# First stage of a one-core decoder layer: x in four column pieces, the first weight chunk split by blocks, identity turns on TensorE ahead of the data

## What is computed

```python
def rmsnorm(x, w):
    xf = x.astype(jnp.float32)
    y = xf * lax.rsqrt(jnp.mean(xf * xf, axis=-1, keepdims=True) + EPS)
    return (y * w.astype(jnp.float32)).astype(x.dtype)
...
    h = x                                     # (1, 256, 2048)
    for l in range(DEPTH):                    # DEPTH = 1
        n = rmsnorm(h, attn_norm_w[l])
        proj = n @ w_in[l]                    # 2048 x 2672
        c_q, c_kv, k_rope, q_nsa, kv_cmp, kv_slc, kv_win, gate_logits = _split_cols(proj, IN_SIZES)
        y_mla = mla_attention(c_q, c_kv, k_rope, positions, ...)
        y_nsa = nsa_attention(q_nsa, kv_cmp, kv_slc, kv_win, gate_logits, ...)
        y = jnp.concatenate([rmsnorm(y_mla, mla_out_norm_w[l]),
                             rmsnorm(y_nsa, nsa_out_norm_w[l])], axis=-1)
        h = h + y @ w_o[l]
        n = rmsnorm(h, mlp_norm_w[l])
        h = h + jnp.square(jax.nn.relu(n @ w_up[l])) @ w_down[l]
    return rmsnorm(h, final_norm_w)
```

## Time and profile before

| what | value |
|---|---|
| median of 3 runs | 1125.73 us (1125.38 to 1125.78) |
| span of the profiled execution, first to last instruction | 1125.1 us |
| TensorE busy | 1091.2 us, 97% of the span |
| VectorE, ScalarE, GpSimd busy | 629.8, 490.7, 94.3 us |
| chain that ended last: TensorE, VectorE, ScalarE | 93%, 3%, 2% |
| DMA | 190.41 MB, 169 GB/s on average |
| mean granted TensorE clock | 0.991 |

### The profile page before, as it was taken

One profiled execution on the slowest core, in us unless ns is written; L12 is line 12 of the kernel. 1 busy time (PEld: TensorE's weight loads), 2 busy tenths in 40 slices (PEclk: granted clock), 3 DMA queues, 4 the chain that ended last, 5 costly groups with the idle time before them and its releaser, 6 DMA issues.

```text
span 1125.1 us, 14165 instructions
## 1 busy us (share of the span) xinstructions
PE 1091.2 (97%) x5544; PEld 893.2 (79%) x5544; DVE 629.8 (56%) x762; ACT 490.7 (44%) x591; POOL 94.3 (8%) x157
## 2 busy tenths in 40 slices
PE   5999899999999999999999999999999999999995
PEld 5889787766666888888888888888888888888784
DVE  3655855566564656546555554554545554654664
ACT  3655344655554454334433433433433433433433
POOL 2135100432121200000000000000000000000002
PEclk9999999899999999999999999999999999999998
DMA  8476563142222555666556655566665665665641
GB/s 295 152 205 204 161 222 102 49 150 76 75 76 82 180 171 176 198 193 194 188 188 186 186 186 186 188 189 187 192 195 185 197 189 190 190 187 186 186 150 75
DMA packets 81807, 190.41 MB, mean 169 GB/s; under 512 B 8598, under 2 KB 20972, under 8 KB 81388
## 3 DMA queue, kind: packets, MB, share of 16 engines
q1 hardware_dynamic: 81772, 189.93, 53.5%
HBM read 187.82 MB, written 2.10 MB: 169 GB/s over the span
## 4 chain that ended last, share of the span: by engine, by line
PE 93%; DVE 3%; ACT 2%; issue 1%; DMA 0%; DVEq 0%; SPq 0%; POOL 0%; ACTq 0%
PE ps L1430 21%; PE ps L1092 17%; PE ps L1093 16%; PE ps L1096 16%; PE ps L1432 11%; PE ps L1249 2%; PE ps L1296 2%; DVE w_lo L723 2%; PE ps L1270 2%; PE ps L1297 1%; PE ps L1247 1%; PE ps L1246 1%; ACT w_hi L506 1%; DMA x_sb<-in_x 0%; PE ps L1286 0%
## 5 line engine op out<-in xcount | busy, mean ns | idle before, releaser
L723 DVE TENSOR_TENSOR w_lo<-raw,w_hi 128x2048 fp32r<-128x2048 f32 (+3 forms) x197 | 405.6, 2062 | 373.4 <-ACT w_hi L513 296.7
L513 ACT ACTIVATE w_hi<-raw 128x2048 fp32r<-128x2048 f32 x120 | 230.2, 1918 | 399.8 <-PE ps L1096 202.1
L1430 PE MATMUL ps<-xT,w_hi 128*128 128x512 f32 x1024 | 361.8, 398 | 1.3 <-DVE h_sb L903 1.0
L1432 PE MATMUL ps<-xT,w_lo 128*128 128x256 f32 x1024 | 287.1, 280 | 0.0
L1430 PEld LDWEIGHTS ps<-xT,w_hi 128*128 128x128 f32 x1024 | 192.3, 188 | 49.2 <-issue 1.3
L1092 PE MATMUL ps<-w_hi,hidT 128*128 128x512 f32 x512 | 200.2, 391 | 2.4 <-issue 2.0
L1093 PE MATMUL ps<-w_lo,hidT 128*128 128x512 f32 x512 | 200.1, 391 | 0.0
L1432 PEld LDWEIGHTS ps<-xT,w_lo 128*128 128x128 f32 x1024 | 193.3, 189 | 0.5
L1096 PE MATMUL ps<-w_hi,hidT 128*128 128x512 f32 x512 | 158.2, 390 | 0.0
L506 ACT ACTIVATE w_hi<-raw 128x1024 fp32r<-128x1024 f32 (+3 forms) x77 | 107.1, 1397 | 85.1 <-PE ps L1096 61.9
L1092 PEld LDWEIGHTS ps<-w_hi,hidT 128*128 128x128 f32 x512 | 96.4, 188 | 23.4 <-issue 2.4
(11 more groups left out here) (245 smaller groups left out, 1021.3 us busy)
## 6 DMA issues: line engine op xcount, KB each, us to landing
raw<-in_w_up SPq DMA_DIRECT2D x64, 1024.0 KB, 5.3
raw<-in_w_down SPq DMA_DIRECT2D x64, 1024.0 KB, 5.5
raw<-in_w_o SPq DMA_DIRECT2D x16, 1024.0 KB, 5.5
raw<-in_w_in SPq DMA_DIRECT2D x8, 1024.0 KB, 5.0
raw<-in_w_in SPq DMA_DIRECT2D x8, 832.0 KB, 7.3
raw<-in_w_in SPq DMA_DIRECT2D x8, 816.0 KB, 4.5
raw<-in_mla_w_uq SPq DMA_DIRECT2D x12, 256.0 KB, 4.5
x_sb<-in_x SPq DMA_DIRECT2D x4, 512.0 KB, 7.0
```

The lines of the kernel that those rows point to most:

```text
L513: act.activation(w_hi[:, j % SPLIT, :], raw[:, j % RAW, :], ACT.Copy).then_inc(hi_done, 1)
L723: return dve.tensor_tensor(dst, src, high.bitcast(F32), ALU.subtract)
L1430: pe.matmul(ps[:, b0 + f, :].rearrange("p (c t) -> p c t", c=2), w_hi[:, slot, w], xT[:, :, k0 + b, :], start=start and b == 0, stop=False)
L1432: m = pe.matmul(ps[:, b0 + f, 0:T], w_lo[:, slot, w], xT[:, 0, k0 + b, :], start=False, stop=stop and b == 3)
```

## The change

SyncE now loads x in four pieces of 512 columns, each with its own semaphore: piece 0 ahead of chunk 0, piece c right after chunk c for c = 1, 2, 3. Chunk 0 is loaded as two DMAs, one for each block of 128 rows, with a semaphore each (`head_in`, and the usual `raw_in`). ScalarE and VectorE split chunk 0 in the same two blocks, between the blocks of x. TensorE has a new helper `keep_warm(n)`, which turns the identity n times into PSUM bank 3, a bank that the first products do not use; it is called with 4, 8 and 8. TensorE takes block 0 of chunk 0 as soon as `head_lo` and `xt_lo` allow and block 1 behind `lo_done`. The sums of squares move from rounds 3 and 4 to 5 and 6, since they need all four pieces, and VectorE's guess moves from round 5 to round 7. The arithmetic stays the same.

```diff
--- before.py
+++ after.py
@@ -210,11 +210,11 @@
-        x_in = sems("x_in0", "x_in1")
+        x_in = sems("x_in0", "x_in1", "x_in2", "x_in3")
         raw_in = sems(*[f"raw_in{n}" for n in range(RAW)])
         prm0_in, prm_in, cst_in, w2_in, h_in, fw_in, stored = sems("prm0_in", "prm_in", "cst_in", "w2_in", "h_in", "fw_in", "stored")
         hi_done, half_hi, lo_done, w_used, w_half = sems("hi_done", "half_hi", "lo_done", "w_used", "w_half")
-        first_done, = sems("first_done")
+        first_done, head_in, head_hi, head_lo = sems("first_done", "head_in", "head_hi", "head_lo")
         act_free, dve_free = sems("act_free", "dve_free")
         pool_c, dve_c = sems("pool_c", "dve_c")
         consts, warm, tables, prm_t, wcols_ok = sems("consts", "warm", "tables", "prm_t", "wcols_ok")
@@ -309,22 +309,28 @@
         @block.sync
         def _(sp):
             sp.dma_start(prm0[:, :], a["attn_norm_w"][0].rearrange("(r p) -> r p", p=P)).then_inc(prm0_in, 16)
-            for t in range(TT):
-                sp.dma_start(x_sb[:, t, 0:D // 2], x_rows[t][:, 0:D // 2]).then_inc(x_in[0], 16)
+            def load_x(q):
+                for t in range(TT):
+                    part = slice(512 * q, 512 * q + 512)
+                    sp.dma_start(x_sb[:, t, part], x_rows[t][:, part]).then_inc(x_in[q], 16)
+
+            load_x(0)
             for c in range(LOOP0):
                 if c >= RAW:
                     sp.wait_ge(lo_done, c - RAW + 1)
                 src, (b, w) = chunk(c)
                 dst = raw[:, raw_slot(c), 0:b * w].rearrange("p (b w) -> p b w", b=b)
-                if len(src) == 1:
+                if c == 0:
+                    for k, landed in enumerate((head_in, raw_in[raw_slot(0)])):
+                        sp.dma_start(dst[:, k, :], src[0][:, k, :]).then_inc(landed, 16)
+                elif len(src) == 1:
                     sp.dma_start(dst, src[0]).then_inc(raw_in[raw_slot(c)], 16)
                 else:
                     for k, piece in enumerate(src):
                         sp.dma_start(dst[:, k, :].rearrange("p (h e) -> p h e", h=piece.shape[1]), piece)\
                             .then_inc(raw_in[raw_slot(c)], 16)
-                if c == 0:
-                    for t in range(TT):
-                        sp.dma_start(x_sb[:, t, D // 2:D], x_rows[t][:, D // 2:D]).then_inc(x_in[1], 16)
+                if 1 <= c <= 3:
+                    load_x(c)
                 if c == RAW - 1:
                     for src, row, n in TABLE:
                         sp.dma_start(prm[row - KT:row - KT + n, :], src).then_inc(prm_in, 16)
@@ -521,18 +527,24 @@
                 act.activation(cT[:, 0, k, :], bank(k % 4, T), ACT.Copy,
                                scale=wcols[:, PRM["c"] + k:PRM["c"] + k + 1]).then_inc(ct_hi, 1)
 
+            def head_split_hi(b):
+                act.wait_ge(raw_in[raw_slot(0)] if b else head_in, 16)
+                act.activation(w_hi[:, split_slot(0), CW * b:CW * b + CW], raw[:, raw_slot(0), CW * b:CW * b + CW], ACT.Copy)\
+                    .then_inc(hi_done if b else head_hi, 1)
+
             act.wait_ge(wcols_ok, 1)
-            for c in range(8):
-                if c:
-                    split_hi(c)
+            x_hi(0)
+            head_split_hi(0)
+            x_hi(1)
+            head_split_hi(1)
+            for c in range(1, 8):
+                split_hi(c)
                 x_hi(2 * c)
                 x_hi(2 * c + 1)
-                if c == 0:
-                    split_hi(0)
-                if c in (3, 4):
-                    t = c - 3
-                    act.wait_ge(x_in[0], 16 * TT)
-                    act.wait_ge(x_in[1], 16 * TT)
+                if c in (5, 6):
+                    t = c - 5
+                    for q in range(4):
+                        act.wait_ge(x_in[q], 16 * TT)
                     if t:
                         act.wait_ge(ssq_ok, t)
                     act.activation(sink[:, :], x_sb[:, t, :], ACT.Square, accum_out=ssq[:, t:t + 1]).then_inc(ssq_ok, 1)
@@ -754,14 +766,17 @@
             dve.wait_ge(prm_t, 1)
             dve.tensor_copy(wcols[:, 0:KT], bank(7, KT)).then_inc(wcols_ok, 1)
             dve.wait_ge(wcols_ok, 1)
-            for c in range(8):
-                if c:
-                    split_lo(c)
+            for b in range(2):
+                x_lo(b)
+                dve.wait_ge(hi_done if b else head_hi, 1)
+                part = slice(CW * b, CW * b + CW)
+                low(w_lo[:, split_slot(0), part], raw[:, raw_slot(0), part], w_hi[:, split_slot(0), part])\
+                    .then_inc(lo_done if b else head_lo, 1)
+            for c in range(1, 8):
+                split_lo(c)
                 x_lo(2 * c)
                 x_lo(2 * c + 1)
-                if c == 0:
-                    split_lo(0)
-                if c == 5:
+                if c == 7:
                     dve.wait_ge(ssq_ok, 2)
                     link(dve.tensor_scalar(ssq[:, 0:2], ssq[:, 0:2], 1.0 / D, EPS, ALU.mult, ALU.add))
                     guess(r1[:, :], ssq[:, 0:2]).then_inc(guessed, 1)
@@ -1121,8 +1136,8 @@
                     pe.wait_ge(wcols_ok, 1)
                 if k >= 4:
                     pe.wait_ge(xt_lo, k - 3)
-                if k == KT // 2:
-                    pe.wait_ge(x_in[1], 16 * TT)
+                if k % 4 == 0:
+                    pe.wait_ge(x_in[k // 4], 16 * TT)
                 for t in range(TT):
                     m = pe.transpose(ps[:, 4 + k % 4, P * t:P * t + P], x_sb[:, t, P * k:P * k + P], ident[:, :])
                 m.then_inc(xt_t, 1)
@@ -1135,16 +1150,31 @@
                 m.then_inc(ct_t, 1)
 
 
+            def keep_warm(n):
+
+                for _ in range(n):
+                    pe.transpose(bank(3, P), ident[:, :], ident[:, :])
+
             pe.wait_ge(consts, 1)
-            pe.wait_ge(x_in[0], 16 * TT)
-            for k in range(3):
-                turn_x(k)
+            keep_warm(4)
             pe.wait_ge(prm0_in, 16)
             pe.transpose(bank(7, KT), prm0[:, :], ident[0:KT, 0:KT]).then_inc(prm_t, 1)
-            turn_x(3)
+            keep_warm(8)
+            for k in range(4):
+                turn_x(k)
+            keep_warm(8)
+            pe.wait_ge(xt_lo, 1)
+            pe.wait_ge(head_lo, 1)
+            for half in range(2):
+                if half:
+                    pe.wait_ge(lo_done, 1)
+                    pe.wait_ge(xt_lo, 2)
+                for t in range(TT):
+                    products(split_slot(0), chunk(0)[1], lambda part, b, t: of_x(part, b, t), LOW, True, False, None, TT * half + t)
             for c in range(8):
-                pe.wait_ge(xt_lo, 2 * c + 2)
-                stream(c, of_x, 2 * c, LOW, c == 0, c == 7)
+                if c:
+                    pe.wait_ge(xt_lo, 2 * c + 2)
+                    stream(c, of_x, 2 * c, LOW, False, c == 7)
                 for k in (2 * c + 4, 2 * c + 5):
                     if k < KT:
                         turn_x(k)
```

## The result

The changed kernel took 1119.24 us (median of 4 executions, 1118.44 to 1121.23), the kernel before beside it 1125.76; the ratio is 0.994, 95% interval 0.9926 to 0.9954. Measured again, it was 1120.19 (4 executions) against 1127.03 for 21 executions of the kernel before, ratio 0.9947 (0.9930 to 0.9963). So the change saves 6.5 to 6.8 us by the medians; 5.4 were forecast. The profiled execution has a span of 1116.8 us and took 1118.58. Of the 39 executions of the kernel before that were timed beside the kernels of this document, none lies between 1125.8 and 1126.8: they come in two groups, and the medians move with how many fall in each. What the groups may be is taken up under the experiments.

A forecast was written before the change was run, and what follows sets the result against it. TensorE, busy 93% of the span, was taken as the bound, so an earlier chunk 1 moves everything: 1125.1 - 5.75 + 0.35 = 1119.7 us span, median 0.6 above, 1120.3 us; range 1118.9 to 1122.8.

The forecast's parts named there:

- pessimistic bound: Start: short 2 KB rows double the time of x's piece 0, adding 1.8 us; chunk 1 lands at 12.5 us.
- optimistic bound: Start: x itself was the slow part, later bytes move at 0.41 MB/us; chunk 1 lands at 10.2 us.
- Chunk 1 at 15.15: Chunk 1's first product waits for its split, later than a warm TensorE (14.2); 20.90 before, gain 5.75 us.
- Rival (a): Start: clock stays low through chunk 0; chunk 1 at 16.3, total 1121.5 us; cold to the end 19.1, 1124.3; chance 0.17.
- Rounds 1 to 7: Rounds after chunk 0: no wait from later loads, cost 0, up to 1 us if the split's cover is gone.
- The norm's factor: Three small VectorE instructions move ahead of the angles: chunk 8 loses 0.6 us, 0.35 stays after chunk 10's wait.
- The sum: Whole kernel: 1125.1 - 5.75 + 0.35 = 1119.7 us span, median 0.6 above it: 1120.3 us.
- (c): Chunk 1 lands late, from short rows or later pieces: 12.5 us, chunk 1 starts at 16.95, total 1122.1; chance 0.10.
- (d): Queued loads served in turn, not in order: chunk 1 lands at 17.4, starts at 21.9, total 1127.1 us; chance 0.03.
- (e): Norm's factor late, holding splits of chunks 10 on: 0.9 or 2.6 us more, total 1120.9 to 1122.6; chance 0.08.
- (f): Change does not take effect, first product held by something unseen; time as before, 1125.7 us; chance 0.05.
- (b): Chunk 1 lands early at 10.2 us, starts at 14.65; total 1119.8, or 1119.5 without norm loss; chance 0.12.

The follow-up runs named there:

- chunk 0 ahead of x: Changed kernel with both blocks of chunk 0 issued ahead of x's first piece; profiled span 1121.2 us, no median given.
- the variant with all parts: Changed kernel with squares and guess back in rounds 3 to 5, 16 identity turns near 1057 us, 16 instead of 8 ahead of x; median 1118.15 us, ratio 0.9923.
- turns in the last gap: Changed kernel with 16 identity turns while TensorE waits for the last hidden block's split, round 1057 us; median 1118.71 us.

## Why the prediction was right, point by point

**x lands at 5.6 us: wrong by 1.0.** It was 6.63. The assumption was that bytes move at the rates of before; from 3 to 6 us they moved at 211 GB/s instead of 280. The prediction's pessimistic bound (x's piece slow, 1.8 us) was the nearer one for x.

**Chunk 1 lands at 10.7: right (10.79).** What x lost, the weights behind it won back: 403 GB/s from 6 to 10. The optimistic bound rested on x being the slow part, and chunk 0 ahead of x showed that to be so. Two errors of opposite sign cancel in this landing; that it came out to 0.1 us is luck.

**First product at 9.2: it was 9.96.** 0.55 of it came with x. The rest is the eight turns behind x, which I had put at no cost: at the low level they ended 0.2 us after `w_lo` was ready. Without the turns the product started at 9.86.

**The turns raise the clock: right**, and shown both ways, by taking them out (chunk 0 in 7.11 us) and by putting them alone into the kernel before (5.01).

**Chunk 1 at 15.15, bound by its split: the number right, its reason half.** Split and TensorE ended together. The forecast 1 us of idle time wasn't there, since chunk 0 started 0.75 us late and began at the low level. The prediction let the clock rise "about halfway through chunk 0" before it mattered. Its own numbers allow less: with the first product at 9.2, 4.96 us of work and half of each microsecond at the low level lost, chunk 1 starts at 15.15 only if the clock is up within 2.0 us. In the variant with all parts the split is the bound (15.07), and moving two x blocks ahead of it gives 14.74. The forecast value is also the early end of what the changed kernel does: 15.15 to 16.22 over four profiles with that start. The first matmul at the high level stands 0.56 us behind the first product in the earliest of them and up to 2.50 behind it in the others (12.49 - 9.99, turns in the last gap). The kernel before has 20.84 to 21.29 in three profiles, so the start gains 4.6 to 6.1 us and the 5.75 was met in this one pair by luck. Rival (a), a clock that rises late, is partly true in some executions.

**Rounds 1 to 7 lose nothing: right**, 4.96 us a round, no wait.

**The norm's factor costs 0.35: mis-sized.** The first half held: 0.56 lost at chunk 8 (34.60 against 34.04), GpSimd 5.4 us with one step of 1.90 beside the split of chunk 8, `rs_ok` 0.7 ahead of ScalarE. But at chunk 10 only 0.1 was left and nothing 185 us on. I had set the waiting time there at the 0.26 us that the row shows as idle. The row's idle time starts at the modelled end of the matmul before; by starts, TensorE could have gone on at 63.9 instead of 64.31, 0.4 to 0.5 earlier. Both experiments on this part, late in the kernel before and early in the changed one, agree.

**The sum: 1.1 us too high for the median, for reasons that worked against each other.** The forecast span was 1119.7, the measured one 1116.8: 0.35 is the norm's factor, the other 2.55 (918.8 - 916.2) stretches at the low clock: about 7 us near 210 in the first profile of before against 3.4, and 3.4 near 1060 against none. The prediction's sum has no term for them, though its own show the one near 1066. And the step from span to time was wrong: I took 0.6 us, from a span of 1125.1 and a median of 1125.73. In every later execution time and span differ by 1.8 us. The profiled execution was one of the slower group (1126.9 by that), the three timed ones were of the faster. The third part is that the profiled execution of the changed kernel (1118.58) lies 0.66 below the median of 1119.24. So the miss of 1.06 is 2.9 less 1.2 less 0.66. The mechanism of the start was right; that the total came this close is in part luck.

**The rivals.** Chunk 1 late (c), served out of turn (d), a late norm factor (e) and no effect (f) did not come; (b), an early landing, did not come either.

## What to carry to other kernels

Where one engine is busy from its first product to its last, the start is worth its full length: list what must be there for the first product, load only that first, and work out landing times from bytes ahead of it. Transposes of an identity in the idle time ahead can have the high clock up at the first product: 24 behind the turns of x did (in the kernel before), and so did 16 ahead of them and 8 behind, while with 8 and 8 it rose 0.56 to 2.50 us after it. They should end before the first product is ready, or they stand in its way. A change of 0.2 to 0.5% needs a look at where the granted clock falls elsewhere in the program, and waiting times should be read from starts, not from the idle time that a row shows.

## What was not expected of the hardware

The granted clock fell late in the program, in stretches of about 3.4, 7 or 10 us that differ between executions of one kernel, costing up to half their length. One place is TensorE's 2.05 us of idle time near 1060 us; sixteen identity turns there left 0.26 us of it in each of the three variants that had them, and none of the three has a low stretch there; of the eleven profiles without them eight have one. The other is near 210 us, where 32 products of 30 columns run (3.76 us in the first profile of the changed kernel): TensorE is busy by the profile, and the clock falls all the same, while they run or up to 1.3 us behind them, in all fourteen profiles. It is low for 3.4 us where it falls behind them and for 7 or 10 where it falls while they run. What sets the moment stays open, and so does whether the turns at the start do; no run here was made on that place.

x's first piece moved at about 205 to 211 GB/s wherever it stood, the data ahead of it or behind it at 374 to 403, and x's third piece, with the same rows, at 411. The cause stays open.
